# A two-layer transformer trunk: the order in which weight chunks take the tiles of x at the norm boundaries, a later sum of squares, and a third halved output tile

## The reference

```python
h = h + weight * gate * rmsnorm(y, g_post)                # y: output of the block before
x = rmsnorm(h, g_pre) * (1 + scale) + shift               # input of the block behind
# feed-forward: y = (silu(x @ w1[:, :F]) * (x @ w1[:, F:])) @ w2,   F = 2752
# mixer:        P = x @ w_in; three branches (band attention, forgetting attention, spatial gating)
#               m = sig(gA)*(oA@W_a) + sig(gB)*(oB@W_b) + sig(gC)*(oC@W_c);  y = m @ w_out
```

## Time and profile before

| | |
|---|---|
| median of 3 runs | 2966.81 us (2965.22 to 2970.06) |
| the profiled execution | 2967.36 us |
| its span in the trace | 2965.6 us |
| mean granted clock of TensorE | 0.992 of full |
| TensorE busy | 2851.5 us, 96% of the span, 21582 matmuls |
| VectorE busy | 1341.4 us, 45% |
| ScalarE busy | 988.4 us, 33% |
| DMA | 109 GB/s mean |
| TensorE's longest total wait | 37.8 us in 26 waits, for x_lo (L1540) |

### The profile page before, as it was taken

The page is one execution under the profiler, slowest core; times in us unless marked ns, Lnnn a source line. Parts: engine busy times, 40 slices in busy tenths (PEclk is TensorE's granted clock), DMA queues, the critical chain, the costliest instruction groups (busy, mean ns, idle before and its releaser), DMA issues.

```text
span 2965.6 us, 49972 instructions
## 1 busy us (share of the span) xinstructions
PE 2851.5 (96%) x21582; PEld 2663.0 (90%) x21582; DVE 1341.4 (45%) x2606; ACT 988.4 (33%) x1861; POOL 108.6 (4%) x202
## 2 busy tenths in 40 slices
PE   7999998999999989999999999989999999999997
PEld 6999998877799989999989999987768999899997
DVE  3444325555444464443274443265554444644423
ACT  4222224344422352222252222244443224422321
POOL 0000000000000000000000000001000000000000
PEclk9999999999999999999999999999999999999998
DMA  5444432333222224442224444323321222122221
GB/s 228 149 150 156 166 107 96 105 108 100 81 86 79 86 79 143 155 143 84 86 86 144 161 159 151 98 84 120 122 94 55 82 81 83 65 86 79 90 82 65
DMA packets 91051, 324.28 MB, mean 109 GB/s; under 512 B 11200, under 2 KB 14304, under 8 KB 90640
## 3 DMA queue, kind: packets, MB, share of 16 engines
q1 hardware_dynamic: 64016, 222.50, 23.2%
q0 software_dynamic: 26816, 98.59, 9.7%
HBM read 310.16 MB, written 11.55 MB: 108 GB/s over the span
## 4 chain that ended last, share of the span: by engine, by line
PE 86%; DVE 6%; ACT 4%; issue 1%; DVEq 1%; DMA 1%; SPq 1%; POOL 0%; ACTq 0%
PE ps L613 76%; PE ps L919 3%; PE ps L703 2%; PE ps L932 1%; PE ps L952 1%; DVE h L1533 1%; DVE w_lo L1408 1%; ACT w_hi L1041 1%; DVEq L1532 1%; DMA w_raw<-in_f 1%; DVE x_lo L1540 1%; DVE z L1531 1%; PE ps L622 1%; ACT x_hi L1125 1%; ACT sig L1353 1%
## 5 line engine op out<-in xcount | busy, mean ns | idle before, releaser
L613 PE MATMUL ps<-x_hi,w_hi 128*128 128x290 f32 (+1 forms) x4256 | 980.4, 305 | 55.7 <-DVE x_lo L1540 37.8
L613 PE MATMUL ps<-x_lo,w_hi 128*128 128x288 f32 (+1 forms) x4256 | 949.5, 298 | 0.0
L613 PE MATMUL ps<-x_hi,w_lo 128*128 128x290 f32 (+1 forms) x4256 | 938.7, 295 | 0.0
L613 PEld LDWEIGHTS ps<-x_hi,w_hi 128*128 128x128 f32 x4256 | 691.1, 189 | 149.6 <-issue 93.8
L613 PEld LDWEIGHTS ps<-x_lo,w_hi 128*128 128x128 f32 x4256 | 701.3, 190 | 0.4
L613 PEld LDWEIGHTS ps<-x_hi,w_lo 128*128 128x128 f32 x4256 | 700.5, 190 | 0.0
L1408 DVE TENSOR_TENSOR w_lo<-w_raw,w_hi 128x1024 fp32r<-128x1024 f32 x386 | 469.5, 1223 | 264.9 <-ACT w_hi L1041 262.8
L1041 ACT CAST w_hi<-w_raw 128x1024 fp32r<-128x1024 f32 x386 | 393.5, 1048 | 98.9 <-DMA w_raw<-in_f 94.6
L613 PE MATMUL ps<-hid_hi,w_hi 128*128 128x288 f32 x1344 | 304.2, 297 | 1.8 <-DVE c_col L1465 1.8
L613 PE MATMUL ps<-hid_hi,w_lo 128*128 128x288 f32 x1344 | 301.9, 295 | 0.0
L613 PE MATMUL ps<-hid_lo,w_hi 128*128 128x288 f32 x1344 | 301.8, 295 | 0.0
(11 more groups left out here) (203 smaller groups left out, 2517.3 us busy)
## 6 DMA issues: line engine op xcount, KB each, us to landing
w_raw<-in_f SPq DMA_DIRECT2D x260, 512.0 KB, 3.5
ada_w<-in_ada POOLq DMA_DIRECT2D x128, 512.0 KB, 5.7
w_raw<-in_gate SPq DMA_DIRECT2D x64, 512.0 KB, 3.5
w_raw<-in_tri SPq DMA_DIRECT2D x42, 512.0 KB, 3.5
decay_s<-f_scratch POOLq DMA_DIRECT2D x8, 1088.0 KB, 8.0
ada_first<-in_ada SPq DMA_DIRECT2D x4, 2048.0 KB, 18.4
w_raw<-in_wout SPq DMA_DIRECT2D x16, 512.0 KB, 3.5
decay_p<-f_scratch POOLq DMA_DIRECT2D x8, 512.0 KB, 6.2
```

What stands on the lines that cost most here:

```text
L613: r = mm(ps[:, 2 * out + b, 0:width], w, xx[:, cols(b)], start=first and n == 0, stop=last and n == 2)
```

## The change

It edits only the order of existing work.

1. `first_group`: chunks 0 and 1 start with tiles 0 and 1 of half 0, and chunk 2 is waited for after that. `sum_of_y` of half 1 comes after tile 2. Before tiles 6 and 7 of half 0, a feed-forward's chunk 3 takes tiles 0 to 5. In half 1 all chunks of the group (four in a feed-forward, three before the projection) take each tile together.
2. `sum_of_h` moves back: into chunk 4 of a feed-forward (behind six of its eight tiles), or behind six tiles of the chunk after the group in the projection.
3. w_out has three halved output tiles, 5, 6 and 7, where it had two. Tile 5 takes accumulator pair 2. Their second halves are evicted one each behind `make_x` of tiles 0, 1 and 2.
4. The splits of weights move to suit: in the boundary chunk 3's from behind tile 5 (ACT) and tile 7 (DVE) to behind tiles 3 and 5; chunk 4's on DVE from the middle of half 1 to the end. In the feed-forward ACT splits chunk 5 after all four raw copies and chunk 6 after `estimate_h`; DVE splits chunk 6 after `norm_of_h`.

```diff
-OUT_PIECES = [(o, BOTH) for o in range(KD - 2)] + [(o, (b,)) for b in BOTH for o in (KD - 2, KD - 1)]
+OUT_HALVED = (KD - 3, KD - 2, KD - 1)
+OUT_PIECES = [(o, BOTH) for o in range(KD - 3)] + [(o, (b,)) for b in BOTH for o in OUT_HALVED]
...
+def y_pair(j, o):
+    if j == 1 and o == KD - 3:
+        return 2, 0
+    return o % 2, o // 2 - (j == 1 and o == KD - 1)
...  first_group (TensorE)
-            for k in range(KD):
-                pe.wait_ge(x_ready.sem, x_ready.done(l, x_index(n, 0, k)))
-                for s in lock:
-                    x_half(l, ph, s, k, 0)
-                if k == 1 and j[0] >= 0:
-                    sum_of_y(*j, 1)
...
+            some(0, (0, 1), (0, 1))
+            chunk_ready(chunk(l, ph, 2))
+            some(0, (2,), (0, 1))
+            some(0, (0, 1, 2), (2,))
+            if j[0] >= 0:
+                sum_of_y(*j, 1)
+            some(0, (0, 1, 2), (3, 4, 5))
+            if more and not first:
+                chunk_ready(chunk(l, ph, 3))
+                some(0, (3,), range(6))
+                some(0, (0, 1, 2, 3), (6, 7))
+            else:
+                some(0, (0, 1, 2), (6, 7))
...
-            for group in ((0, 1), *((s,) for s in (*lock[2:], *rest))):
...
+            some(1, range(4) if more else range(3), range(KD))
...  ffn (TensorE)
-            if l or n:
-                pe.wait_ge(alt_taken.sem, alt_taken.done(l, ab == "b"))
-                sum_of_h(*((l, n - 1) if n else (l - 1, 2)), 2)
+            def late_sum(t):
+                if t == KD - 2:
+                    pe.wait_ge(alt_taken.sem, alt_taken.done(l, ab == "b"))
+                    sum_of_h(*((l, n - 1) if n else (l - 1, 2)), 2)
...  before_pairs (TensorE)
-            sum_of_h(l, 0, 3)
-            project(l, 1, 0, KD)
+            project(l, 1, 0, KD - 2)
+            sum_of_h(l, 0, 3)
+            project(l, 1, KD - 2, KD)
...  boundary (ScalarE)
-                        if k in (1, 5, 7):
+                        if k in (1, 3, 7):
                             split_hi()
-                        if k == 2:
-                            for p in pieces(j, 1):
-                                done(1, PIECES[j][p][0])
-                                evict(l, j, p)
+                        late = pieces(j, 1)
+                        if 0 <= k - 3 + len(late) < len(late):
+                            p = late[k - 3 + len(late)]
+                            done(1, PIECES[j][p][0])
+                            evict(l, j, p)
...  ffn_up (VectorE)
                 split_lo()
+                norm_of_h(*((l, 1) if ab == "b" else (l - 1, 2)), 2)
                 split_lo()
-                norm_of_h(*((l, 1) if ab == "b" else (l - 1, 2)), 2)
...  boundary (VectorE)
             x_low(nl, n, 0, 5)
+            split_lo()
             new_h(l, j, 0, 4)
             norm_of_y(l, j, 1)
             x_low(nl, n, 0, 6)
             x_low(nl, n, 0, 7)
-            split_lo()
...
             x_low(nl, n, 1, 1)
-            split_lo()
             x_low(nl, n, 1, 2)
...
+            if j:
+                split_lo()
             add_squares_of_h(l, j)
+            if not j:
+                split_lo()
```

More of the change, by code:

```diff
@@ new lines, in first_group, with some @@
+            first = (l, n) == (0, 0)
+            def some(b, group, ks):
+                for k in ks:
+                    pe.wait_ge(x_ready.sem, x_ready.done(l, x_index(n, b, k)))
+                    for s in group:
+                        r = x_half(l, ph, s, k, b)
+                        if b and k == KD - 1:
+                            r.then_inc(chunk_done.sem, 1)
+            for s in (0, 1):
+                chunk_ready(chunk(l, ph, s))
+                pair_free(l, ph, s, 0)
+            some(0, (0, 1), (0, 1))
@@ new lines, in first_group @@
+            chunk_ready(chunk(l, ph, 2))
[10 more added lines that the diff above has]
+                some(0, (0, 1, 2), (6, 7))
+            if first:
+                first_ada(FIRST_MODS[1])
+                chunk_ready(chunk(l, ph, 3))
+                some(0, (3,), range(KD))
+                pe.wait_ge(start_shift.sem, start_shift.done(0, 0))
@@ L793, in out_products @@
         def out_products(l):
-            for i in range(KD - 2):
-                whole_chunk(l, "out", i, i % 2, i // 2, m_hi, m_lo, columns,
+            for i in range(KD - 3):
+                whole_chunk(l, "out", i, *y_pair(1, i), m_hi, m_lo, columns,
                             gate=(lambda t: pe.wait_ge(prod_lo.sem, prod_lo.done(l, KF + t))) if i == 0 else None)
             for b in BOTH:
-                for i in (KD - 2, KD - 1):
-                    c = chunk(l, "out", i)
+                for i in OUT_HALVED:
+                    c, (p, group) = chunk(l, "out", i), y_pair(1, i)
                     if b == 0:
                         chunk_ready(c)
-                        pair_free(l, "out", i % 2, i // 2)
+                        if p < 2:
+                            pair_free(l, "out", p, group)
                     for k in range(KD):
-                        if b and i == KD - 2 and k == 4:
+                        if b and i == KD - 3 and k == 5:
                             sum_of_y(l, 1, 0)
-                        r = split_tile(i % 2, c, k, m_hi[:, k, :], m_lo[:, k, :], columns, k == 0, k == KD - 1, (b,))
+                        r = split_tile(p, c, k, m_hi[:, k, :], m_lo[:, k, :], columns, k == 0, k == KD - 1, (b,))
                     r.then_inc(chunk_done.sem if b else y_half.sem, 1)
@@ L1055, in ffn_up @@
                 first_raw(l, ab)
+                split_hi()
+                split_hi()
             for i in range(KF - 1):
@@ L1100, in evict @@
             o, halves = PIECES[j][p]
-            n = PIECE_AT[j] + p
+            n, out = PIECE_AT[j] + p, y_pair(j, o)[0]
             act.wait_ge(y_added.sem, y_added.free(l, n))
             if halves == BOTH:
-                A(two(sq[:, n % 2, 0:TOK]), pair[o % 2], ACT.Square).then_inc(sq_ready.sem, 1)
+                A(two(sq[:, n % 2, 0:TOK]), pair[out], ACT.Square).then_inc(sq_ready.sem, 1)
             else:
-                A(sq[:, n % 2, columns(halves[0])], pair[o % 2][:, halves[0], :], ACT.Square).then_inc(sq_ready.sem, 1)
+                A(sq[:, n % 2, columns(halves[0])], pair[out][:, halves[0], :], ACT.Square).then_inc(sq_ready.sem, 1)
             for b, g, part in spans(halves):
-                r = A(z[:, o, part], pair[o % 2][:, b, part.start - b * HALF:part.stop - b * HALF],
+                r = A(z[:, o, part], pair[out][:, b, part.start - b * HALF:part.stop - b * HALF],
                       ACT.Identity, scale=post_gate[:, j, o, g:g + 1])
             if 1 in halves:
-                r.then_inc(acc_free[o % 2].sem, 1)
+                if out < 2:
+                    r.then_inc(acc_free[out].sem, 1)
             elif o == KD - 1:
@@ L1545, in boundary @@
         def boundary(l, j):
-            last_acc = acc_free[1].done(l, GROUP_AT[("f2a", "out", "f2b")[j]][1] + KD // 2 - 1)
+            last_acc = acc_free[1].done(l, GROUP_AT[("f2a", "out", "f2b")[j]][1] + y_pair(j, KD - 1)[1])
             for p in pieces(j, 0):
```

42 lines of the change are left out of this document (13 added, 29 removed).

## The result

The changed kernel takes 2978.8 us (median of 10 runs, 2974.5 to 2983.45), the kernel before 2967.93 (10 runs, 2965.22 to 2971.24). The ratio is 1.0035, with a 95% interval of 1.0025 to 1.0045: slower by 10.9 us, which is more than the 0.2% that the prediction calls a difference. The profiled execution has a span of 2977.3 us against 2965.6.

The account below looks back on a forecast made before the run. TensorE, busy 96% of the span, was taken to be held at boundaries by the serial chain behind sum_of_h. Dependencies -0.3 and clock +13.5 - 1.6 gave +11.6 us: 2978.5 us, range 2962 to 2985.

Parts of the forecast that it names:

- Part 1: Boundary 1, up to the last tile of x: estimate 0.9 us later, last x_lo +0.7 us (-0.2 to +1.3).
- Part 2: Boundaries 1 and 4, to L862: sum behind 36 matmuls, L862 +1.4 us each, TensorE idle nearly 7 us.
- Part 3: Boundary 3: group ends 4.7 us earlier, but chunk 6's split joins the chain; +0.9 us, stall about 5.6 us.
- Part 4: Boundaries 2 and 5: third halved tile brings h 2.8 us earlier; -3.1 us in boundary 2, -2.8 in 5.
- rival that more stalls lose the clock: Waits for tile 6 (boundaries 1, 4) and restarts in 2, 5 cost up to 2 us each: 2986; chance 0.09.
- Part 5: The start: chunk 0 done 5.7 us later and chunk 5's load waits for it; +1.9 us (1.4 to 2.7).
- Part 6: Clock: stalls of 5.6 to 6.8 us in all five boundaries cost 2.7 us each, +13.5; boundary 4's loss today, -1.6.
- rival that the group's end decides: All boundaries gain the group's earlier end: -26 us, 2941; chance 0.14 together with a milder form at 2957.
- rival that the clock holds: Clock holds at the new stalls, or slow stretch is short: -1.9 us, 2965, no change by measurement; chance 0.15.

Follow-up runs that it names:

- second run: Changed kernel with sum_of_y of half 1 behind the first 12 matmuls of the group, not the first 27: 2968.41 us, ratio 1.0002.
- first three runs: Changed kernel with, one each: chunk 6's split ahead of the estimate (2975.88 us); sum_of_y behind 12 matmuls (2968.41 us); idle 222-column matmuls in long stalls (2971.66 us).
- the version without fillers: Changed kernel with sum_of_y of half 1 behind 12 matmuls and both splits ahead of norm_of_h, no idle matmuls: 2963.60 us, ratio 0.9989.
- the one with fillers: Changed kernel with sum_of_y behind 12 matmuls, both splits ahead of norm_of_h, and idle 288-column matmuls in the five long stalls: 2955.39 us, ratio 0.9960.

## Why the prediction was right, and where its sizes were off

The forecast was 2978.5 and the kernel takes 2978.8. The mechanism was as forecast: a long stall at the end of the chain behind `sum_of_h` in all five boundaries, and the lower clock behind each. That the number fits to 0.3 us is luck, as the parts show. I set each part against the profile by the lag of the same point of the program, before against after (what each boundary adds to it):

| | before | after | adds | forecast |
|---|---|---|---|---|
| start, to the end of f1a | 465.96 | 466.35 | +0.4 | +1.9 |
| boundary 1, clock included | 545.25 | 550.00 | +4.4 | +4.1 |
| boundary 2 | 1116.31 | 1121.80 | +0.7 | -0.4 |
| boundary 3 | 1560.77 | 1569.50 | +3.2 | +3.6 |
| boundary 4 | 2013.66 | 2024.64 | +2.3 | +2.5 |
| boundary 5 | 2806.98 | 2819.19 | +1.2 | -0.1 |

With -0.5 behind that, these make the 11.7 by which the span grew. Each point is the start of the same piece in the chains of both, the last one where the next equal piece stands in both.

- **Part 1** held. The estimate in boundary 1 came 1.74 us later, 1.35 of it beyond the start's 0.4, against +0.9; the sum behind 27 matmuls did 1.2 of it, as the second run shows by its reverse. The gain of 0.3 in front of them didn't come: TensorE restarted at 485.58, 0.2 later than before by the lag, since ScalarE had first to split a chunk whose load had only just landed, and the eviction stood behind that:

```profile
482.90 1.06 ACT L1063 CAST w_hi<-w_raw 128x1024 fp32r<-128x1024 f32 x1 [0.67 <-DMA w_raw<-in_tri]
```

 The last x_lo came at 511.24, +1.41 against the earlier trace rows, less 0.4 from the start is +1.0, forecast +0.7:

```profile
511.24 0.65 DVE L1566 SCALAR_TENSOR_TENSOR x_lo<-h,pre_scale,x_hi 128x224 fp32r<-128x224 f32 x2 [0.30 <-ACT x_hi L1150]
```

- **Part 2** held in kind. `sum_of_h` at 518.80 and L884 at 527.87 are 2.4 and 2.2 later than the earlier trace rows, less 0.4 gives 1.8 for L884, forecast 1.4; in boundary 4 it is 1.4. The stall of nearly 7 us is there, with 6.5 measured.
- **Part 3** held. In boundary 3's chain 120 matmuls run unbroken from the last wait on, the last 36 of them chunk 4's:

```profile
1521.78 16.64 PE ps L621 x120
1538.42 0.98 PE ps L665 x4
...
1553.87 14.64 PE ps L621 x96
```

 The group's own 84 end at 1521.78 + 84 / 120 x 16.64 = 1533.4; less the lag of 5.5 at this point that is 1527.9 against 1532.09 before, 4.2 earlier, forecast 4.7. None of it arrived: the sum is at 1538.42, less 5.5 1532.9, chunk 6 starts 1.6 later (1553.87 against 1546.81, less 5.5), forecast 0.9, and boundary 3 added 3.2 with its clock, forecast 3.6.
- **Part 4** was mis-sized: it is the term that failed. The estimate in boundary 5 came 1.6 us earlier by the lag (2535.16 against 2525.77, less 11.0), not 3.3, and chunk 6 restarted 1.4 and 1.0 earlier in boundaries 2 and 5, not 3.1 and 2.8. The restart behind the eviction came after a wait of 2.7 us for z, 2.5 forecast, and I had let its matmuls run at full clock. They did not: 27 took 5.34 us, where the same 27 take 3.81 in the other boundaries. That is 1.5 us in each of boundaries 2 and 5, and explains what these two added beyond forecast (+1.1 and +1.3). The run with the third halved tile alone shows the same, 4.15 us for 18. It is part of the rival that more stalls lose the clock, which I had given 0.09; its other part, the waits of some 3 us in boundaries 1 and 4, did not lose it in this trace.
- **Part 5** came out at +0.4 against +1.9 between the two traces, but most of the difference is the trace of the kernel before. Chunk 0 was done at 64.23, forecast 65.4, and the freed pair came at 80.45 + 0.15 us, forecast 82.2:

```profile
64.23 0.16 ACT L1108 COPY c_col<-ps 128x2 f32<-128x2 f32 x1 [13.23 <-PE ps L621]
```

 The windows of the same work at the start, in the kernel before and then in the run with `sum_of_y` behind the first tile of x, whose start is the same:

```profile
40.00:44.00 4.00, 4.00 (x21) 4.00 (x20) 4.00 (x12) 4.00 (x14) 0.00 (x0) 0.60 0.02 7
...
40.00:44.00 4.00, 4.00 (x32) 3.99 (x31) 4.00 (x12) 4.00 (x14) 0.00 (x0) 1.00 0.02 7
```

 The clock fell in the one and not in the other, and the first piece of the table stands at 465.96 and 464.32. Of the traces with full clock in this window, the three with the order of the kernel before have that point at 464.3 to 464.6, and the changed kernel, the first three runs and the version without fillers at 465.8 to 466.4: the change costs the start some 1.5 us, within the bounds of 1.4 to 2.7. Over the runs the first whole chunks start anywhere from 78.8 to 82.3 us.
- **Part 6** held in kind, and its size was 2.4 too high. In boundary 1 the lag grows from 2.16 at L884 to 4.75 behind the 96 matmuls, 2.6; boundary 4's block is 0.14 shorter (13.91 for 14.05), 2.45; boundaries 2 and 3 take 15.09 and 14.64 where the same block took 12.96 before, 2.1 and 1.7; boundary 5 took 2.2 more for its next 1776 matmuls (238.28 and 236.07). That makes 11.1 against 13.5. The Trainium skill (TensorE: Matmul & The Clock Gate, Terms) counts the penalty as throttled time times the share of the clock taken away. The trace agrees to 0.3 us: 6 us at 0.54 give 2.8, where 2.6 were measured in boundary 1, and 5.4 us at 0.56 give 2.4, where boundary 2's block lost 2.1.

The errors cancel. The dependencies, up to the restarts behind the long stalls, came to +2.7 us where -0.3 was forecast (1.5 too high at the start, 3.0 too low at the restarts behind the eviction, 1.5 too low in the chains), and the clock behind the stalls to 9.5 us where 11.9 was. The number is closer than its working, and the parts are what to judge it by.

What the runs settled is the price of each cause. The place of `sum_of_y` is 10.4 us, for 15 matmuls of which the change itself had put in 9, and the split in the chain 2.9; together they gave 15.2 by the medians (2978.80 to 2963.60) and 13.6 by the ratios, about their sum. Filling the five long stalls is worth another 8.2. The traces with and without fillers differ by 10.0 us from the end of the start on (2.7, 1.6, 1.5, 1.9 and 2.3 in boundaries 1 to 5), close to the 11.1 that I read from the blocks; the one with fillers had begun 2.1 us later, as its clock fell to 0.68 from 40 to 44 at the start. The rival that the group's end decides is refuted: in boundary 3 the group ended 4.2 us earlier and TensorE then waited 5.5 us for c_col. The rival that the clock holds is refuted by 0.54, 0.56 and 0.50 behind the stalls.

What stays open: how the 3.6 us of half 1 in boundaries 1 and 4 divide between its groups and the sum's place, whether the order of half 0 is worth anything by itself (no run has it alone), and what makes the clock fall at a short wait in one trace and not in another.

## What to carry to other kernels

When a wait is taken off the bounding engine, follow the serial chain behind it to the next place where that engine stops: here 13.6 us less at x_lo came back as 28.1 us more at c_col and L884. A long stall costs a second time: behind each of the five TensorE ran at half clock for microseconds, 1.7 to 2.6 us of loss. Breaking it up into short waits with matmuls between them is no sure cure: it gave 3.6 us in each of two boundaries and nothing in three, where the clock fell among the short waits. Filling it with idle matmuls worked in all five. And since one such fall is worth 1.5 us and comes and goes where the order is the same, a difference of 1 or 2 us between two traces is not yet an effect; compare boundary by boundary and look at the clock in each. Last, the place of a two-matmul reduction in an in-order queue can be worth more than the grouping of a hundred: put it at the first place where its input is there.

## What the runs showed of the hardware that was not expected

- A matmul of 222 columns, loading its own weights, saved less than its share of columns against one of 288: 28 of them took 3.38 us and 44 took 5.07, 0.11 to 0.12 us each, and 96 of 288 columns take 12.75, 0.133 each.
- A wait of 2.7 us for z in boundaries 2 and 5 was followed by the lower clock (27 matmuls in 5.34 us), and so was one of 2.2 us behind 28 fillers. A wait of 2.8 us for x_lo in boundary 1 was not: its windows read 1.00. In the run with fillers of 222 columns, whose order is the same up to there, the same wait of 2.8 us was (0.50 from 498 to 501). In the kernel before, waits of at most 1.9 us left the clock at 1.00 in boundary 1; in boundary 4 it read 0.50 from 1970 to 1972, and again behind a wait of 1.7 us for L862 that is as long in boundary 1, where it read 1.00 behind it. The length of a stall alone does not tell which; no run here tells what does.
- Matmuls that compute nothing, put into a stall, made the kernel 8.2 us faster.
